# Attention in units of two heads, gate rows as two fp32r parts, weights first in the loads, and eight stages that enter without a barrier

## The reference

```
first_block, for l in 0, 1:
    x += even_mixer(norm(x))      # l = 0: 8 softmax heads of 64 (2 key heads) and 4 two-way mLSTM heads of 128
      or odd_mixer(norm(x))       # l = 1: 8 neighbourhood heads of 64, 4 differential heads of 128
    x += memory_cross_attention(norm(x), norm(mem))     # 4 heads of 128, q and k normalised
    x += conv_ffn(norm(x))                              # 2816 wide
second_block, for l in 0, 1:
    x += 0.5 * swiglu(norm(x))
    x += hybrid_mixer(norm(x))    # 6 heads with forget gates ("fox"), 5 sparse ones (top 64 keys, "dsa"),
                                  # 5 stick-breaking ones, all of 64; three gates of 1024; merged @ w_out
    x += memory_cross_attention_2(norm(x), norm(mem_2)) # 4 heads of 128, no norm of q and k
    x += 0.5 * swiglu(norm(x))
return norm(x)
```

## Time and profile before

| | before |
|---|---|
| median of 3 runs | 2589.35 us |
| the profiled execution's own time | 2590.67 us |
| its span in the trace | 2588.8 us |
| mean granted clock of TensorE | 0.952 |
| TensorE busy | 2394.8 us, 93% |
| VectorE busy | 1603.0 us, 62% |
| ScalarE busy | 1096.6 us, 42% |

### The profile page before, as it was taken

One profiled execution on the slowest core, in us unless ns is written; L12 is line 12 of the kernel. 1 busy time (PEld: TensorE's weight loads), 2 busy tenths in 40 slices (PEclk: granted clock), 3 DMA queues, 4 the chain that ended last, 5 costly groups with the idle time before them and its releaser, 6 DMA issues.

```text
span 2588.8 us, 41000 instructions
## 1 busy us (share of the span) xinstructions
PE 2394.8 (93%) x17744; PEld 2239.1 (86%) x17744; DVE 1603.0 (62%) x2326; ACT 1096.6 (42%) x1329; POOL 34.8 (1%) x60
## 2 busy tenths in 40 slices
PE   6989999998799999999998799999999988889997
PEld 5868899986689999999967688999999967688997
DVE  4565587755457786656557646666666446655654
ACT  4435454533444444335334345334334324445332
POOL 1300000000000000000000000000000000000000
PEclk8889999998799999999989899999999989899999
DMA  8523245441134555555521344555556522244552
GB/s 256 173 70 132 96 165 194 164 146 59 56 129 167 187 172 179 186 176 153 180 78 54 113 163 136 176 177 182 177 179 179 172 66 77 68 151 145 175 185 82
DMA packets 318901, 373.79 MB, mean 144 GB/s; under 512 B 23647, under 2 KB 289651, under 8 KB 317571
## 3 DMA queue, kind: packets, MB, share of 16 engines
q1 hardware_dynamic: 313715, 353.32, 41.7%
q0 software_dynamic: 3424, 11.50, 1.5%
q10 hardware_dynamic: 1584, 6.36, 0.7%
HBM read 361.97 MB, written 9.18 MB: 143 GB/s over the span
## 4 chain that ended last, share of the span: by engine, by line
PE 77%; DVE 11%; ACT 6%; issue 2%; PEld 2%; DMA 1%; DVEq 0%; PEldq 0%; ACTq 0%
PE bank L727 20%; PE bank L730 20%; PE bank L728 20%; DVE wlo L1503 3%; ACT whi L1140 3%; PE bank L757 2%; PE bank L758 2%; PE bank L737 2%; PE bank L968 2%; PE bank L1017 2%; PE bank L761 2%; PE bank L897 1%; PE bank L1004 1%; ACT x_hi L1186 1%; DVE xT L1532 1%
## 5 line engine op out<-in xcount | busy, mean ns | idle before, releaser
L727 PE MATMUL bank<-x_hi,wlo 128*128 128x256 f32 (+1 forms) x4432 | 1143.9, 290 | 24.3 <-DVE wlo L1503 8.3
L728 PE MATMUL bank<-x_lo,whi 128*128 128x256 f32 (+1 forms) x4432 | 1131.4, 287 | 0.0
L1503 DVE TENSOR_TENSOR wlo<-raw,whi 128x2048 fp32r<-128x2048 f32 (+2 forms) x344 | 762.0, 2224 | 324.4 <-ACT whi L1140 324.2
L1140 ACT ACTIVATE whi<-raw 128x2048 fp32r<-128x2048 f32 (+2 forms) x344 | 638.9, 1860 | 719.4 <-PE bank L730 651.5
L727 PEld LDWEIGHTS bank<-x_hi,wlo 128*128 128x128 f32 (+1 forms) x4432 | 869.5, 196 | 51.5 <-issue 31.5
L728 PEld LDWEIGHTS bank<-x_lo,whi 128*128 128x128 f32 (+1 forms) x4432 | 870.2, 196 | 0.0
L730 PE MATMUL bank<-x_hi,whi 128*128 128x256 f32 x4432 | 710.9, 286 | 0.0
L730 PEld LDWEIGHTS bank<-x_hi,whi 128*128 128x128 f32 x4432 | 615.7, 195 | 4.6 <-issue 0.7
L757 PE MATMUL bank<-x_hi,wlo 128*128 128x256 f32 x544 | 154.8, 315 | 46.5 <-DVE xT L1532 19.8
L757 PEld LDWEIGHTS bank<-x_hi,wlo 128*128 128x128 f32 x544 | 111.3, 205 | 52.2 <-issue 32.0
L758 PE MATMUL bank<-x_lo,whi 128*128 128x256 f32 x544 | 144.1, 295 | 0.0
(11 more groups left out here) (225 smaller groups left out, 1986.9 us busy)
## 6 DMA issues: line engine op xcount, KB each, us to landing
raw<-in_ffn_w_gu SPq DMA_DIRECT2D x88, 1024.0 KB, 5.1
raw<-in_ffn_w_down SPq DMA_DIRECT2D x66, 1024.0 KB, 5.2
raw<-in_ffn_w_up SPq DMA_DIRECT2D x44, 1024.0 KB, 5.1
raw<-in_w_in SPq DMA_DIRECT2D x42, 1024.0 KB, 5.2
raw<-in_ca_w_kv SPq DMA_DIRECT2D x16, 1024.0 KB, 5.1
raw<-in_od_w_in SPq DMA_DIRECT2D x12, 1024.0 KB, 5.1
raw<-in_ev_w_in SPq DMA_DIRECT2D x10, 1024.0 KB, 5.3
raw<-in_w_in SPq DMA_DIRECT2D x20, 512.0 KB, 5.2
```

What stands on the lines that cost most here:

```text
L727: eng.matmul(out, a[1], b[0], start=first and i == 0, stop=False, skip_group_check=True)
L728: eng.matmul(out, a[0], b[1], start=False, stop=False, skip_group_check=True)
L1140: eng.activation(whi[s % SETS][:, 0:ch["n"]], raw[i % SLOTS][:, 0:ch["n"]], ACT.Copy).then_inc(S["weights_hi"], 1)
L1503: eng.tensor_tensor(wlo[s][:, 0:n], full[:, 0:n], whi[s][:, 0:n].bitcast(F32), ALU.subtract).then_inc(S["weights_split"], 1)
```

## The change

1. **Units of heads.** Softmax and stick-breaking heads of 64 features go two at a time, one on each partition half (`small_heads`), cross attention's 128-feature heads two at a time (`large_heads`). The even and odd mixers have 4 units instead of 8 heads, fox 3, dsa 3, stick 3, cross attention 2 instead of 4. PSUM banks are taken in pairs (`bank_pairs`): one pair for the scores of a unit, one for its transposed probabilities. The scores of unit i wait for the exponentials (or, with bias, the maxima) of unit i-1. TensorE's order is scores(i), fill, values(i-2), turn(i-1); VectorE's is maxima(i), evacuation, normalise(i), fill, output(i-2). Every reduction, copy and output handles the whole unit in one instruction; exponentials and normalising keep one per head and query tile.
2. **Gate rows** become two fp32r parts, `rr`: ScalarE copies the high part to partitions 0.. (and 64..), VectorE's new `row_parts` subtracts the low part to partitions 32.. (and 96..). One fp32r product with a one-hot column over 64 partitions (`pick`) takes the place of the float32 ones.
3. **Splits.** Within a fill slot the weights are split one chunk past the units, not two; a new `filled(st)` at the end of each heads and attention stage does the second. The units' slots are numbered anew.
4. **Start.** SyncE loads chunks 0, 1 and 2 before any parameter. x is first on ScalarE's queue, then the constants and norm_mix; mem comes last. VectorE copies xT.
5. **Barriers.** Four places in the code (eight stages that run: the second half of w_out in the even and odd mixers, w_out of two hybrid mixers, w_o of four cross attentions) join without a barrier; they wait for `att_done`, for the head norms or for the merged tiles. The hybrid w_out's parts are made during the merge stage (`feeds`).

```diff
-            bufs, lag = {"softmax": (4, 2), "stick": (4, 3)}.get(kind, (2, 2))
             dual = kind in ("mlstm", "difference")
-            stage("attention", att=kind, units=units, u0=number("att", len(units)), bufs=bufs, lag=lag,
-                  sc=[banks[i] for i in ((0, 1, 6, 7) if dual else (0, 1))],
-                  pt=[banks[i] for i in ((2,) if dual else (2, 3))], ob=[banks[i] for i in ((3,) if dual else (6, 7))], **more)
+            stage("attention", att=kind, units=units, u0=number("att", len(units)), z0=number("stick", len(units) if kind == "stick" else 0), bufs=2, lag=2,
+                  sc=[banks[i] for i in (0, 1, 6, 7)] if dual else bank_pairs[0], pt=[banks[2]] if dual else bank_pairs[1],
+                  ob=[banks[3]] if dual else banks[6:8], **more)
...
-            attention("softmax", [small_head(o, 0, 4, h, (h // 4) * HD, h, kh=h // 4, bias=None) for h in range(8)],
-                      fill={0: (M[4], M[3]), 2: (M[5], M[4]), 4: (M[6], M[5]), 6: (M[6] + 1, M[6]), 8: (M[6] + 1, M[6] + 1)})
+            attention("softmax", [small_heads(o, 0, 4, (h, h + 1), 0, 0, kv=lambda h: h // 4) for h in range(0, 8, 2)],
+                      fill={0: (M[4], M[3]), 1: (M[5], M[4]), 2: (M[6], M[5]), 3: (M[7], M[6])})
...
-                      fill={0: (H[0], M[7]), 1: (H[1], H[0]), 3: (H[2], H[1])}, tanh=M[7] + 1)
+                      fill={"pre": (H[0], M[7]), 0: (H[1], H[0]), 1: (H[2], H[1]), 3: (H[3], H[2])}, tanh=M[7] + 1)
...
-            linear(residual_half(wo, b, 0), then=then)
+            linear(residual_half(wo, b, 0), parts=parts_of_heads(n_of["att"] - 2), then=then, join=True)
...
-                      fill={0: (G[4], G[3]), 2: (G[5], G[4]), 4: (G[6], G[5]), 6: (G[7], G[6])}, tanh=G[5])
+                      fill={0: (G[4], G[3]), 1: (G[5], G[4]), 2: (G[6], G[5])}, tanh=G[5])
...
             load(0)
+            load(1)
+            load(2)
...
+            def in_units(st):
+                units, sc, pt, ob, u0 = st["units"], st["sc"], st["pt"], st["ob"], st["u0"]
+                stick = st["att"] == "stick"
+
+                def scores(i):
+                    un = units[i]
+                    if i:
+                        eng.wait_ge(S["att_z" if stick else "att_exp" if un["heads"][0]["bias"] is None else "att_max"], st["z0"] + i if stick else u0 + i)
+                    for t in range(QT):
+                        n, at = keys(un, t), (t * P if stick else t * SEQ)
+                        for j, h in enumerate(un["heads"]):
+                            m = eng.matmul(sc[:, j, at:at + n], h["q"][:, t * P:(t + 1) * P], h["k"][:, 0:n], start=True, stop=h["row"] is None)
...
+                    for k in range(QT):
+                        for j, h in enumerate(un["heads"]):
+                            q0 = k * P if un.get("causal") else 0
+                            at = turned_at(un, q0 // P, k)
+                            m = eng.matmul(ob[i % 2][h["pb"]:h["pb"] + h["d"], h["col"] + q0:h["col"] + SEQ], h["v"][:, k, :],
+                                           pair_probsT[:, j, at:at + SEQ - q0], start=k == 0 and h["col"] == 0, stop=k == QT - 1, skip_group_check=True)
...
-                    split_upto(units_of[emit_end - 1]["chunk"] + 2)
+                    split_upto(units_of[emit_end - 1]["chunk"] + 1)
                     evac_upto(evac_end)
+
+            def filled(st):
+
+                if st["fill"]:
+                    split_upto(units_of[max(emit_end for emit_end, _ in st["fill"].values()) - 1]["chunk"] + 2)
...
+                if st["gates"]:
+                    row_parts(st["gates"])
                 if st.get("mem_scale") is not None:
                     mem_scaled(st["mem_scale"], 0, 16)
+                filled(st)
+
+            def row_parts(st):
+
+                n, w = (4, 2 * SEQ) if st["cell"] else (6, SEQ)
+                eng.wait_ge(S["rows_hi"], st["n"] + 1)
+                for p0 in (0, HD) if not st["cell"] else (0,):
+                    eng.tensor_tensor(rr[p0 + 32:p0 + 32 + n, 0:w], post_bank[0][0:n, 0:w], rr[p0:p0 + n, 0:w].bitcast(F32), ALU.subtract)
```

569 lines of the change are left out of this document (332 added, 237 removed).

## The result

The changed kernel took 2597.62 us, the median of 8 runs from 2594.84 to 2602.41, beside 2589.37 us (8 runs) for the kernel before: a ratio of 1.0036, with a 95% interval of 1.0026 to 1.0047. It is slower by about 8 us, where I had forecast 2587 us and no change to speak of. The time lies in the range, the direction is wrong.

A forecast was written before the change was run, and what follows sets the result against it. TensorE, busy 93% of the span, was taken as the bound, so only its waits, lower clock or own work count. Terms -5 + 4.3 - 11.9 + 21 - 17.8 + 6 = -3.4 from 2590.67 gave 2587 us; range 2562 to 2604.

The forecast's parts named there:

- Start, -5: Start of the kernel: reordered loads and VectorE's copies shorten the wait for the second low part, -2 to -9 us.
- Even mixer, +4.3: Even mixer: +9.4 us ahead of the scores, -6.8 in the softmax, +1.7 in the mLSTM stage.
- Odd mixer, -11.9: Odd mixer: softmax -7.0 us, second head norms -1.9, difference stage -2.2, last barrier -0.8.
- First block's cross attentions, +21: Two unfilled cross attentions: serial chain of two units +7.5 us each, lower clock +3 each; bounds +15 to +31.
- Hybrid mixers, -17.8: Two hybrid mixers, -8.9 us each: fox -6.5, dsa +3.5, stick -2.4, w_out -3.5.
- Stick: ... -2.4: Hybrid mixer's stick stage: earlier scores after z's copy and a moved fill unit covering part of the chain, -2.4 us.
- w_out ... -3.5: Hybrid w_out: its 3.97 us wait for low parts shrinks because they are made within the merge stage, -3.5 us.
- Hybrid cross attentions, +6: Two cross attentions in the hybrid block: two serial units leave 2 us more open, clock 1 us, +3 each.
- The joins: Places joined without a barrier: -0.8 us for the odd mixer's last barrier, from a wait at the joins of 1.07 us.
- The slower rival: Cross attentions' serial two-unit chain takes the clock with it: +11.6 us over the sum, 2602 us; chance 0.18.
- The column halves: Softmax values: column halves don't overlap, a unit's values still take 1.84 us, 6.9 us more, 2594 us; chance 0.05.
- The rule of evacuation as the bound: Softmax stages: VectorE's and ScalarE's PSUM reads set the pace, so -6.8 and -7.0 don't come; 2601 us; chance 0.05.

The follow-up runs named there:

- e5: The kernel before with only w_o of the four cross attentions joining without a barrier and taking the heads' outputs as they come: 2587.01 us, ratio 0.9999.
- e6: The kernel before with the changed order of loads alone, ScalarE still copying xT: 2586.06 us, ratio 0.9995.
- e2: The changed kernel with all four cross attentions head by head again on two score banks, w_o still joined: 2564.24 us, ratio 0.9913.
- e3: The changed kernel with cross attention as four units of one head, scores still in one bank: 2583.43 us, ratio 0.9987.

## Why the prediction was wrong

- **Start, -5.** -6.0 in the trace. The size was right, the reason mostly not: I gave it to the loads and counted VectorE's copies among the rest. The loads alone are worth 1.4 us by the median, the copies moved off ScalarE about 4 to 5.
- **Even mixer, +4.3.** +9.4 ahead of the scores, exactly the step's working (row parts, memory rows, split), then -5.3 for -5.1, and -1.4 behind it; +2.7 in all. Right in this pair of traces. In two others of the kernel before (e5, e6) the softmax and mLSTM stretch took 94.3 us and not 97.1, so of the -5.3 only 2.5 are sure. The softmax by itself went from 48.8 to 46.2 us although a unit of 48 products, 5.8 us long, runs at its end now that ran in the mLSTM stage before; without it I estimate -8.5 for the step's -6.8.
- **Odd mixer, -11.9.** -17.1 in this trace, -15.4 in the middle one of the seven with the same code. The term was 3 to 5 us short: the softmax gained 9.7 us here (7.0 in the step), the difference stage 5.2 (2.2), where the splits ahead of the probabilities went.
- **First block's cross attentions, +21.** 9.5 + 1.5 + 10.4 = +21.4. Right in sum, by some luck. I gave 3 us each to a lower clock behind the stage, which did not come: from w_o to the next norm the clock is 1.00, the FFN's is 0.99 in both traces, and its 1.5 us are a longer wait, which isn't the change's (below). The chain itself was 21.9 us, at 0.75, and not 20.1, because my sum left out that TensorE makes the first unit's late values before it turns the second unit's probabilities.
- **Hybrid mixers, -17.8: the step that failed.** -9.2. Fox took 41.2 us (41.8 in the step's working), dsa 34.3; but "Stick: ... -2.4" was 38.4 against 38.1 with the moved unit, +0.3, and "w_out ... -3.5" was nothing: from the merge's start to w_out's it is 42.5 us for 42.6 before. For the stick stage the runs show why: I had priced the split at the stage's end in the even mixer and in cross attention, +2.2 each, and left it out here, where it stands ahead of three barriers, and the unit in the stick stage found its low part 5.22 us late. Two ahead again, that stage took 33.9 us, and the hybrid mixers alone gave 16.9 us. For w_out the split order is not the reason (43.6 us with two ahead). Its wait of 3.97 us did go, but inside the merge two waits for VectorE's evacuation came, 0.87 and 1.82 us, and the same products were busy 37.67 us for 36.37, at a clock of 0.88 for 0.91. Why they came stays open.
- **Hybrid cross attentions, +6.** +10.4. "Two serial units leave two more us open" was read off a stage with fill; the values' wait alone is 3.81 us there. Head by head they are 4.1 us shorter each.
- **The joins** were priced at 0.8 and at the wait of 1.07 us. In the changed kernel they are worth 19 us. This did not spoil the sum, because the terms were taken stage by stage against a chain that ends with the values; it would have, had I been asked for the joins alone.

The terms of the trace add up to +4.1 us, 7.5 over my -3.4: 8.6 from the hybrid mixers, 4.4 from their cross attentions, 1.7 from the final norm and 0.4 from the first block's cross attentions, less 1.0 at the start, 5.2 in the odd and 1.6 in the even mixer; the rest is rounding. The other 4 us up to the 8 of the medians are that the profiled execution was 2.8 us below its median, and the one before 1.3 above. The measured 2597.6 us is nearer to three rivals, 2594, 2601 and 2602, than to my 2587, but none of their mechanisms is what happened. **The slower rival** at 2602 us named the clock, and the first block's cross attentions cost what the forecast said, with a clock of 1.00 behind them. **The column halves** (2594) do overlap. **The rule of evacuation as the bound** (2601), from the Trainium skill (TensorEngine Tiling (Array Packing), PSUM Bottleneck), would have taken the two softmax gains away; the page names a fourfold speedup of TensorE for it, and here two heads go at once. The gains came, by 5.3 us with the mLSTM stage and by 9.7. In fox alone TensorE's end waited for VectorE, 9.44 us, and there the top-k rounds and the split were in its queue.

Two of the prediction's own signs were wrong by a slip: "memory rows begin after 101 us" and "the first scores at 110 to 111" leave out the start's own -5 us. The rows began at 95.90 and the scores at 104.72, which even trips "before 105 us", a sign of faster, although the step's +9.4 came in full.

Left open: why each hybrid mixer was 2.4 us shorter when only the cross attentions were edited (e2, e3), and how e3's 6 us divide between the score bank and the loop's order.

## What to carry to other kernels

When a change saves work on the busiest engine, add up what it puts in front of each barrier on the others; here 49 us of products went and 55 us of waits came. Splitting, copying or preparing for the next stage at the end of a stage is not hidden where a barrier follows: price it at every place where it occurs, not at the two where it was noticed. Larger units paid here in the softmax stages of small heads, where other work fills the wait between their steps. In a short attention with two units they make a serial chain, and head by head with two banks was better, by 9 us a stage without fill and still by 4 with it.
